# HGRN projections: six blocks as seven half products, with weight sums made by accumulating DMAs

## The reference, cut to what matters

```python
q, f, i, g = the four 1024-wide column groups hq, hf, hi, hg of h @ w_in      # 8 heads of 128
# S_t = diag(f_t) S_{t-1} + k_t^T v_t (k_t = 1 - f_t), o_t = S_t^T q_t, in chunks of 64 tokens
o = hgrn2_chunked(silu(q), 1 - f, i, log f)
y_h = (rmsnorm(o per head) * silu(g)) @ w_branch_hgrn * sigmoid(h @ w_gate_h)
```

## Time and profile before

| what | value |
|---|---|
| median of 3 runs | 2753.91 us (2753.42 to 2761.96) |
| the profiled execution | 2753.67 us, span 2751.8 us |
| mean granted TensorE clock | 0.991 |
| TensorE busy | 98% of the span |
| VectorE, ScalarE, GpSimd busy | 46%, 23%, 2% |
| DMA into weight_ring, 2 MB | 7.8 us median from issue to landing |
| the HGRN branch | about 1174 to 1605 us of the span |

### The profile page before, as it was taken

The page is one execution under the profiler, slowest core; times in us unless marked ns, Lnnn a source line. Parts: engine busy times, 40 slices in busy tenths (PEclk is TensorE's granted clock), DMA queues, the critical chain, the costliest instruction groups (busy, mean ns, idle before and its releaser), DMA issues.

```text
span 2751.8 us, 29095 instructions
## 1 busy us (share of the span) xinstructions
PE 2694.8 (98%) x11586; PEld 1798.4 (65%) x11586; DVE 1260.3 (46%) x2498; ACT 638.5 (23%) x1460; POOL 60.5 (2%) x116
## 2 busy tenths in 40 slices
PE   8999899998999999999999999999999999999999
PEld 4445547656468888746556765656565685688886
DVE  5733333445234456425463426464664451344564
ACT  2123221246210000132342122434242202000001
POOL 0000000000000000000000001010110000000000
PEclk9999899999999999999999999999999999999999
DMA  4211012100122222220110131121111321222222
GB/s 154 83 40 62 31 63 81 62 31 1 61 92 92 77 77 92 77 92 31 62 61 31 68 118 48 45 77 47 62 47 62 147 91 61 92 92 91 75 80 77
DMA packets 120447, 194.91 MB, mean 71 GB/s; under 512 B 5148, under 2 KB 61272, under 8 KB 119416
## 3 DMA queue, kind: packets, MB, share of 16 engines
q1 hardware_dynamic: 118848, 180.82, 19.3%
q0 software_dynamic: 1344, 12.19, 1.1%
q10 hardware_dynamic: 120, 0.03, 0.0%
HBM read 185.69 MB, written 7.34 MB: 70 GB/s over the span
## 4 chain that ended last, share of the span: by engine, by line
PE 96%; DVE 2%; ACT 1%; issue 1%; DMA 0%; ACTq 0%; DVEq 0%
PE psum L507 19%; PE psum L504 15%; PE psum L2270 14%; PE psum L417 9%; PE psum L437 8%; PE psum L2252 8%; PE psum L402 6%; PE psum L1140 2%; PE psum L2124 2%; PE psum L1160 2%; PE psum L635 1%; PE psum L390 1%; PE psum L1148 1%; PE psum L2481 1%; PE psum L2347 1%
## 5 line engine op out<-in xcount | busy, mean ns | idle before, releaser
L2270 PE MATMUL psum<-weight_ring,h_t 128*128 128x512 f32 x896 | 406.6, 596 | 0.5 <-issue 0.5
L560 DVE TENSOR_TENSOR arena<-arena,psum 128x512 f32<-128x512 f32 x179 | 122.9, 687 | 348.8 <-PE psum L507 287.6
L2270 PEld LDWEIGHTS psum<-weight_ring,h_t 128*128 128x128 f32 x896 | 162.0, 191 | 162.3 <-issue 161.1
L417 PE MATMUL psum<-h_t,weight_ring 128*128 128x512 f32 x544 | 235.6, 593 | 2.2 <-DVEq L2997 0.8
L2252 PE MATMUL psum<-h_t,weight_ring 128*128 128x512 f32 x512 | 235.3, 601 | 1.7 <-ACT arena L2655 1.4
L507 PE MATMUL psum<-h_t,weight_ring 128*128 128x256 f32 x1024 | 228.2, 379 | 0.0
L504 PE MATMUL psum<-weight_ring,arena 128*128 128x256 f32 x992 | 222.8, 382 | 1.5 <-ACT arena L2692 1.5
L507 PEld LDWEIGHTS psum<-h_t,weight_ring 128*128 128x128 f32 x1024 | 194.5, 190 | 27.5 <-issue 1.3
L504 PEld LDWEIGHTS psum<-weight_ring,arena 128*128 128x128 f32 x992 | 190.0, 192 | 28.4 <-issue 2.2
L417 PEld LDWEIGHTS psum<-h_t,weight_ring 128*128 128x128 f32 x544 | 102.7, 190 | 131.1 <-issue 129.1
L437 PE MATMUL psum<-weight_ring,h_t 128*128 128x512 f32 x384 | 170.4, 605 | 3.2 <-ACT h_t L1227 2.0
(11 more groups left out here) (408 smaller groups left out, 3311.4 us busy)
## 6 DMA issues: line engine op xcount, KB each, us to landing
weight_ring<-in_ffn_w_in_dram SPq DMA_DIRECT2D x44, 1024.0 KB, 7.5
weight_ring<-in_w_in_dram SPq DMA_DIRECT2D x20, 2048.0 KB, 7.8
weight_ring<-in_ffn_w_out_dram SPq DMA_DIRECT2D x8, 2048.0 KB, 7.8
weight_ring<-in_w_in_even_dram SPq DMA_DIRECT2D x7, 2048.0 KB, 8.2
weight_ring<-in_w_in_odd_dram SPq DMA_DIRECT2D x5, 2048.0 KB, 7.8
weight_ring<-in_w_in_dram SPq DMA_DIRECT2D x8, 1024.0 KB, 6.9
weight_ring<-in_w_branch_gdn_dram SPq DMA_DIRECT2D x4, 2048.0 KB, 9.0
weight_ring<-in_ffn_w_out_dram SPq DMA_DIRECT2D x4, 1536.0 KB, 6.8
```

Of the source, the lines that this page charges most:

```text
L417: last = pe.matmul(bank, slot[:, k, c:c + P], act[:, k, :], start=(k == 0), stop=(k == KD - 1))
L560: ins = dve.tensor_tensor(out, other, bank, op)
L2270: last = pe.matmul(bank, act[:, k, t * P:(t + 1) * P], slot[:, k, :], start=(k == 0), stop=(k == KD - 1))
```

## The change

Six of the blocks (hq 0, hi 0, hg 0, hq 1, gate_h 0, gate_h 1) are computed as seven half products in the order p4, p1, p2, p5, p6, p7, p3. The sums of the weight quarters are not made by VectorE but inside the ring slot, by four DMAs of 512 KB on POOL's queue that add into their destination: w21 += w11; and a chain w22 += w12 (from DRAM), w11 += w22, w12 += w11, each released by the product that last reads the old value (p4, p1, p2) and by the link before it. The sums of the activations are made once by VectorE (`dve_streamed_tokens`, four operations on 1024 columns, the same four sums as in `dve_token_sums` with other signs, ahead of the forget tiles), put into the arena, and copied by a DMA of 2 MB into `x_res`, whose content is spilled to DRAM at the stage's start and reloaded at the end of gate_h 1 (`pool_hgrn`). POOL does all this before it issues the load of gab_w. `weights_used` counts at p5 instead of at the block's first matmul.

The first block is woven between the forget tiles: three tiles of hf 0, three products of hq 0, the fourth tile, four products. hi 0 and hg 0 are drawn in units of one product by `HGRN_UNITS`: three before level 0, then 1, 2, 2, 2, 2, 1, 1 after the levels. hq 1, gate_h 0 and gate_h 1 use three banks of their own (5, 6, 7), the states get the other five (0 to 4) instead of six; four products come at once and then one each before the third and the fourth pair of updates and one after it (gate_h 1: four, the o_t transposes, three). The products are negated and copied (p4, p1, p5) by ACT or summed (p2, p6, p7, p3) by VectorE at fixed places of their programs; Silu and Sigmoid are applied afterwards to whole halves in the arena. The blocks hf 0, hf 1, hi 1 and hg 1 stay as they are. The diff, cut to its core:

```diff
+STREAMED = ("p4", "p1", "p2", "p5", "p6", "p7", "p3")
+SUMMED = {"p5": 1, "p6": 2, "p3": 3}
+def pe_seven_streamed(K, pe, key, act, tokens, token_major, among=None):
+    blk = K.next_block()
+    n = KD // 2
+    w11, w12, w21, w22 = quarters(K, blk, KD)
+    t1, t2, t4, t3 = sums_view(tokens, KD)
+    x11, x21, x22 = act[:, 0:n, LOW], act[:, n:KD, LOW], act[:, n:KD, HIGH]
+    sides = {"p4": (w22, t4), "p1": (w11, x11), "p7": (w21, t3), "p2": (w12, x21), "p5": (w22, t1), "p6": (w11, t2),
+             "p3": (w12, x22)}
+    K.streamed_at[key[1:]] = blk, K.count("blocks_streamed")
+    at = K.streamed_at[key[1:]][1]
+    pe.wait_ge(K.weight_landed[blk % SLOTS], K.landed_at[blk])
+    for name in STREAMED:
+        left, right = sides[name]
+        bank = K.next_bank((key, name), among)
+        if K.turn((key, name)) > 1:
+            pe.wait_ge(K.free_of((key, name)), K.turn((key, name)) - 1)
+        if name == "p7":
+            pe.wait_ge(K.difference_landed, 16 * at)
+        if name in SUMMED:
+            pe.wait_ge(K.chain_landed, 48 * (at - 1) + 16 * SUMMED[name])
+        for q in range(2):
+            for k in range(n):
+                out, first, last = bank[:, q * HALF:(q + 1) * HALF], k == 0, k == n - 1
+                if token_major:
+                    ins = pe.matmul(out, right[:, k, q * P:(q + 1) * P], left[:, k, :], start=first, stop=last)
+                else:
+                    ins = pe.matmul(out, left[:, k, q * P:(q + 1) * P], right[:, k, :], start=first, stop=last)
+                if name == "p5" and q == k == 0:
+                    ins.then_inc(K.weights_used, 1)
+        ins.then_inc(K.full_of((key, name)), 1)
+        yield
...
+def pool_quarter_sums(K, pool, key):
+    blk, at = K.streamed_at[key[1:]]
+    w11, w12, w21, w22 = quarters(K, blk, KD)
+    (_, src), = K.blocks[blk]
+    pool.wait_ge(K.weight_landed[blk % SLOTS], K.landed_at[blk])
+    pool.dma_start(w21, w11, accum_op=ALU.add).then_inc(K.difference_landed, 16)
+    pool.wait_ge(K.full_of((key, "p4")), K.turn((key, "p4")))
+    pool.dma_start(w22, src[:, 0:KD // 2, HALF:2 * HALF], accum_op=ALU.add).then_inc(K.chain_landed, 16)
+    pool.wait_ge(K.full_of((key, "p1")), K.turn((key, "p1")))
+    pool.wait_ge(K.difference_landed, 16 * at)
+    pool.wait_ge(K.chain_landed, 48 * at - 32)
+    pool.dma_start(w11, w22, accum_op=ALU.add).then_inc(K.chain_landed, 16)
+    pool.wait_ge(K.full_of((key, "p2")), K.turn((key, "p2")))
+    pool.wait_ge(K.chain_landed, 48 * at - 16)
+    pool.dma_start(w12, w11, accum_op=ALU.add).then_inc(K.chain_landed, 16)
...
+def act_streamed(K, act, key, name, quarter, base):
+    n = K.streamed_at[key[1:]][1]
+    out = {"p4": quarter(1, 0), "p1": base, "p5": quarter(1, 1)}[name]
+    key = (key, name)
+    act.wait_ge(K.full_of(key), K.turn(key))
+    if n > 2 and name == "p1":
+        act.wait_ge(K.base_done, n - 2)
+    bank = pair(K.bank(key)) if len(out.shape) == 3 else K.bank(key)
+    act.activation(out, bank, ACT.Copy, scale=-1.0).then_inc(K.free_of(key), 1)
...
+def dve_streamed(K, dve, key, name, quarter, base):
+    c11, c12, c21, c22 = (quarter(c, t) for c, t in ((0, 0), (0, 1), (1, 0), (1, 1)))
+    at = (key, name)
+    if name == "p2":
+        dve.wait_ge(K.free_of((key, "p1")), K.turn((key, "p1")))
+        dve.wait_ge(K.full_of(at), K.turn(at))
+        dve.tensor_tensor(c11, pair(K.bank(at)), pair(base), ALU.subtract).then_inc(K.free_of(at), 1)
+        dve.wait_ge(K.free_of(at), K.turn(at))
+    if name == "p6":
+        dve_product(K, dve, key, "p6", base, base)
+    if name == "p7":
+        dve_product(K, dve, key, "p7", c12, pair(base), ALU.subtract)
+        dve.wait_ge(K.free_of((key, "p5")), K.turn((key, "p5")))
+        dve.tensor_tensor(base, base, c22, ALU.add).then_inc(K.one_more("dve"), 1)
+        dve.wait_ge(K.steps["dve"], K.step_n["dve"])
+        dve.tensor_tensor(c22, c22, c12, ALU.add).then_inc(K.one_more("dve"), 1)
+        dve.wait_ge(K.free_of((key, "p4")), K.turn((key, "p4")))
+        dve_add(K, dve, c21, c12)
+    if name == "p3":
+        dve.wait_ge(K.full_of(at), K.turn(at))
+        dve.tensor_tensor(c12, pair(K.bank(at)), pair(base), ALU.subtract).then_inc(K.free_of(at), 1)
+        dve.wait_ge(K.free_of(at), K.turn(at))
+        dve.tensor_copy(K.stat[:, 76:77], K.stat[:, 77:78]).then_inc(K.base_done, 1)
...
-    pe_feature_major(K, pe, (s, "hf", 0), K.h_t, [0, P, 2 * P, 3 * P], blk)
-    blk = K.next_block()
-    pe.wait_ge(K.weight_landed[blk % SLOTS], K.landed_at[blk])
-    pe_feature_major(K, pe, (s, "hq", 0), K.h_t, [0, P, 2 * P, 3 * P], blk)
+    queries = pe_seven_streamed(K, pe, (s, "hq", 0), K.h_t, V["tokens_a"], False)
+    for n in range(4):
+        pe_forget_tile(K, pe, (s, "hf", 0), K.h_t, blk, n)
+        if n == 2:
+            K.token_sums["pe"] += 1
+            pe.wait_ge(K.tokens_summed, K.token_sums["pe"])
+            pe_take(queries, 3)
+    pe_take(queries, 4)
     for g in range(2):
-        blk = K.next_block()
-        pe.wait_ge(K.weight_landed[blk % SLOTS], K.landed_at[blk])
-        pe_token_major(K, pe, (s, "hi", g), K.h_t, 512, blk=blk, tiles=HGRN_FIRST[g])
-        rest = HGRN_REST[g]
+        if g == 0:
+            inner = pe_hgrn_stream(K, pe, s, V)
+            pe_take(inner, HGRN_UNITS[0])
+        else:
+            blk = K.next_block()
+            pe.wait_ge(K.weight_landed[blk % SLOTS], K.landed_at[blk])
+            pe_token_major(K, pe, (s, "hi", g), K.h_t, 512, blk=blk, tiles=HGRN_FIRST)
...
         if g == 0:
-            fill = pe_stream_feature(K, pe, (s, "hq", 1), K.h_t)
+            pe.wait_ge(K.tokens_moved, 16)
+            fill = pe_seven_streamed(K, pe, (s, "hq", 1), K.h_t, V["tokens_s"], False, HIGH_THREE)
         else:
-            fill = pe_stream_token(K, pe, (s, "gate_h", 0), K.h_t)
-        pe_take(fill, 2 * KD)
+            fill = pe_seven_streamed(K, pe, (s, "gate_h", 0), K.h_t, V["tokens_s"], True, HIGH_THREE)
+        pe_take(fill, 4)
...
-            fill = pe_stream_token(K, pe, (s, "gate_h", 1), K.h_t)
-            pe_take(fill, 2 * KD)
+            fill = pe_seven_streamed(K, pe, (s, "gate_h", 1), K.h_t, V["tokens_s"], True, HIGH_THREE)
+            pe_take(fill, 4)
...
-    pe_take(fill, 2 * KD)
+    pe_take(fill, 3)
...
-HGRN_FIRST = ((0, 1), (0, 1, 2))
-HGRN_REST = ((("hi", 2), ("hi", 3), ("hg", 0), ("hg", 1), ("hg", 2), ("hg", 3)),
-             (("hi", 3), ("hg", 0), ("hg", 1), ("hg", 2), ("hg", 3)))
+HGRN_UNITS = (3, 1, 2, 2, 2, 2, 1, 1)
+HGRN_FIRST = (0, 1, 2)
+HGRN_REST = (("hi", 3), ("hg", 0), ("hg", 1), ("hg", 2), ("hg", 3))
+def pe_hgrn_stream(K, pe, s, V):
+    for name in ("hi", "hg"):
+        yield from pe_seven_streamed(K, pe, (s, name, 0), K.h_t, V["tokens_a"], True)
...
-    K.banks_in_turn = WORK_BANKS
+    K.banks_in_turn = LOW_FIVE
...
-        if h == 3:
-            pe_take(fill, KD)
+        if h > 1:
+            pe_take(fill, 1)
...
-    pe_take(fill, KD)
+    pe_take(fill, 1)
...
+HGRN_COPIES = ((("hi", "p4"), ("hi", "p1")), (("hi", "p5"),), (), (("hg", "p4"),), (("hg", "p1"),), (("hg", "p5"),), (), ())
+HGRN_SUMS = {0: (("hi", "p2"),), 2: (("hi", "p6"), ("hi", "p7")), 3: (("hi", "p3"),), 4: (("hg", "p2"),),
+             5: (("hg", "p6"),), 6: (("hg", "p7"), ("hg", "p3"))}
+HGRN_BASES = (("hq", 0), ("hi", 0), ("hg", 0), ("hq", 1), ("gate_h", 0), ("gate_h", 1))
...
+            for p in ("p4", "p1", "p5"):
+                act_hgrn_part(K, act, s, V, "hq", 0, p)
+        act.wait_ge(K.base_done, 4 if g else 1)
+        raw = V["gate_y"][:, :, 0:T] if g else V["q"]
+        act.activation(V["q"], raw, ACT.Silu).then_inc(K.hgrn_queries, 1)
...
+        beside = ("gate_h", 0) if g else ("hq", 1)
+        act_hgrn_part(K, act, s, V, *beside, "p4")
...
+        act_hgrn_part(K, act, s, V, *beside, "p1")
+        act_hgrn_part(K, act, s, V, *beside, "p5")
...
+        if g == 0:
+            dve_hgrn_sums(K, dve, s, V, "hq", 0, "p2", "p6", "p7", "p3")
+        dve.wait_ge(K.hgrn_queries, 1 + g)
...
+        dve_hgrn_sums(K, dve, s, V, *beside, "p6", "p7", "p3")
+        if g == 0:
+            dve.wait_ge(K.gates_open, 1)
...
+    dve_hgrn_sums(K, dve, s, V, "gate_h", 1, "p2")
...
+    dve_hgrn_sums(K, dve, s, V, "gate_h", 1, "p6")
+    dve_weight_sums(K, dve, K.branch_blocks["y_h"], KD, V["weights0"], None)
+    dve_hgrn_sums(K, dve, s, V, "gate_h", 1, "p7", "p3")
+    dve_weight_sums(K, dve, K.branch_blocks["y_h"] + 1, KD, V["weights1"], None)
...
+    dve.wait_ge(K.x_reloaded, 16)
...
+def pool_hgrn(K, pool, s, V):
+    pool.wait_ge(K.lb_shifted, 1)
+    pool.dma_start(K.x_dram, K.x_res[:]).then_inc(K.x_spilled, 16)
+    for n, (name, g) in enumerate(HGRN_BASES):
+        pool_quarter_sums(K, pool, (s, name, g))
+        if n == 0:
+            pool.wait_ge(K.x_spilled, 16)
+            pool.dma_start(K.x_res[:], V["tokens_a"]).then_inc(K.tokens_moved, 16)
+    last = ((s, "gate_h", 1), "p3")
+    pool.wait_ge(K.full_of(last), K.turn(last))
```

(40 more changed lines are left out.)

61 lines of the change are left out of this document (53 added, 8 removed).

## The result

The changed kernel takes 2766.94 us (median of 16 runs, 2759.00 to 2780.11) beside 2761.27 us for the kernel before (16 runs, 2753.39 to 2762.43): a ratio of 1.0034, 95% interval 1.0021 to 1.0047. The forecast was 2742.0, in a range of 2734 to 2757. The profiled execution took 2764.37 us around a span of 2762.5, 10.7 us more than the 2751.8 before.

What follows compares the result with a forecast made beforehand. The prediction took TensorE, busy 98% of the span, to bound the kernel; 19.8 - 2.85 - 0.9 - 1.3 - 3.0 = 11.75 us saved from 2753.7 gave 2742.0 us, in a range of 2734 to 2757.

Steps and rivals of the forecast that it cites:

- d: Accumulating DMAs: time of one link from releasing product to landing, taken as 5.1 us, costing TensorE 0 us of waits.
- four such loads: Weight loads of hg 0, hq 1, gate_h 1 and y_h 0, issued at a p5: 0 us each.
- hi 0's load: Weights of hi 0, stretched by the token-sum copy from 7.8 to 12 us or so: TensorE waits 0, at most 2.
- (c): Rival: accumulating links are slow; at d = 9.0 waits of 11.8 us take all the gain; chance 0.17.
- (b): Rival: clock falls in level 0's wait, 0 to 3 us more, or d is 7 to 8.5; about 2747; chance 0.20.
- My sums for slow links: Link waits over the six blocks: 11.8 us at d = 9.0, 26 at d = 10, 54 at 11.7.
- The estimate of 4.4 us for d: One link by the Trainium skill: about 2.0 us plus bytes over 436 GB/s, at half rate for an add.
- The gain: Seven half products take 24.17 us a block instead of 27.47: 3.30 us saved in each of six blocks, 19.8 us.
- Level 0: Before level 0's scores TensorE waits 2.85 us for factors from VectorE and ACT.
- Bank of hq 1: Before hq 1's first product TensorE waits 0.9 us for bank 5, which VectorE frees late.
- States: After the last updates only one product precedes the outputs: TensorE waits 0.6 us twice, 1.3 us with hand-over included.
- Tail: In gate_h 1 and before y_h's first product, TensorE waits for banks: 0.35, 1.7 and 0.9, together 3.0 us.

Runs made afterwards that it cites:

- Experiment 1: Changed kernel with weights_used counted at p3 instead of p5 in hq 1 and gate_h 0: 2756.42 us, ratio 1.0001.
- experiment 5: Changed kernel with three load releases moved: hq 1 to p3, gate_h 0 to level 5's first scores, gate_h 1 to the first output matmul: 2752.66 us, ratio 0.9978.
- experiment 2: Changed kernel with eight useless matmuls before the second-link wait in hq 1 and gate_h 0: 2763.67 us, ratio 1.0031.
- experiment 7: Changed kernel with experiment 5's releases, token-sum copy behind hi 0's chain, banks beginning with 6, hq 0's sums before the second differences: 2739.64 us, ratio 0.9931.
- experiment 3: Changed kernel with the 2 MB copy of the token sums moved from behind hq 0's chain to behind hi 0's: 2764.1 us, one execution.

## Why the prediction was wrong

**The step that failed** is "With d = 5.1 every link lands in time: 0 us". A link left alone was close to it, 5.4 to 6.4 us. But d was taken as one number for all 18 links, while it depends on which other transfers run beside it. I had the release of the load in hand: I wrote of four such loads that they are issued at a p5, "with 17 us or more to their use", and put them at 0; that of hf 1, issued at hq 1's p5, isn't even in the list. I never asked what the load does to the chain that runs at the same moment, though I did ask it the other way round for hi 0's load and the copy. In hq 1, gate_h 0 and gate_h 1 the second link is issued within a microsecond of p5 and has the least room of all. The price was 13.8 us of waits and 6.9 us of products at the low clock, together 20.7: the whole gain and 0.9 more. Experiment 1 removes the cause in two blocks and gets 14.5 us back in them; experiment 5 does it in all three, and experiment 2 shows that the slow products come from the pause.

**The rivals.** The outcome is nearest to (c): the waits stand in the three blocks it named, and those blocks' links at 11.6 to 13.2 us are past its point of 9.0. Its reason was wrong, though: no slow add, no piece size, no slow wake-up of POOL, since the same links take 5.4 to 6.4 us elsewhere. Rival (b) supplied the other third: its row of a slow restart after 3.3 us of waiting was the right row, and I had applied it to level 0's wait alone, at 1.4 us; behind each link wait it came to 1.8 to 2.7. My sums for slow links are too low: in hq 1, gate_h 0 and gate_h 1 the third link, with 21 to 23 us and 20.8 of room by my own count, is not or not fully in them. With it, d = 9.0 costs some 17 us and not 11.8, and the gain is gone from about d = 8.5 on; d = 11.7 costs over 60 and not 54. At d = 5.1 it changes nothing. The estimate of 4.4 us for d was too low as well: no accumulate took under 5.4.

**What held.** The gain, nearly: 19.8 us was worked out from products in unbroken rows. With all causes out of the way (experiment 7) the stage is 16.7 shorter, 0.9 of the rest being waits and some 2 the products that stand alone. **Level 0**: the time at which its factors are ready was right (experiment 3); the wait of 2.85 was 2.51 there, and 0.44 in the changed kernel, with the load's 1.82 in front of it. The two together are 2.26. **hi 0's load**: "at most 2, and that would hide in the next wait" is what happened, in this profile, though the load took 15.1 us and not "12 or so". In other profiles the wait was 1.89 and 2.01 with a slow product behind it (5.41), or 3.32 to 4.15 with one of 6.2 to 6.6; that hid only in part. **Bank of hq 1**: 0.9, measured 0.94. **States**: 0.6 twice, measured 0.35 twice. **Tail**: 3.0; with the link wait in front it can't be seen in the changed kernel, since ACT and VectorE catch up meanwhile, and it measured 2.7 once that was gone.

**The sum.** My 2742.0 is near the 2739.64 of experiment 7, and that is luck: that kernel also lacks the 6.75 us of waits that I had priced for level 0, the bank and the tail, so the same sum gives 2753.7 - 19.8 + 1.3 = 2735.2 for it. The kernel that I forecast is that of experiment 5, with only the failed step mended. It took 2752.66, some 10 us more than my figure, and 4.6 less than the kernel before in its session, where I had 11.75. In its profile the stage is 5.6 us over the 419.45 that I forecast (431.20 - 11.75), most of it hi 0's load and the slow product behind it, 6.6 us where I had 2.85 for level 0. That profile took 2762.40 us, the slowest of its ten: 6.1 less than the profiled execution of the kernel before in the stage, 8.3 more ahead of it and 6.6 more behind it, between 1905 and 2110 us, by falls of the clock. The median of before that the forecast stood on, 2753.91, was itself the lower of that kernel's two usual times, which no view of one profile could show.

## What to carry to other kernels

When a change makes work depend on a chain of DMAs, list every transfer that starts during the chain, and above all those that the change itself moves there; ask of each not only whether it is in time for its own use, but whether it delays the chain. Here a slot's release could be moved to the last link, or ahead of the block, and nothing became late. And price a wait of TensorE of 3 to 5 us at its length plus about 2 us for the restart: 1.6 to 2.9 in the rows here.
